# Seven block products for eight in the down projection of a two-layer transformer kernel

## The chip, the cores and the metric

The kernel runs on one core of a Trainium2 chip. The metric is the time of one execution on the device in microseconds (us), lower is better. The kernel before takes 3250.4 us, the median of three runs (3247.45 to 3253.56).

## What is computed

The model is a block of two stages. The first stage (mixers and a mixture of experts) is not touched. The second stage is two layers of the same form over x with 512 tokens and 1024 columns, all in 32-bit floats:

```python
def hybrid_layer(x, cond, ...):
    ...                                   # norm, four kinds of mixing heads, projection w_out
    x = x + gate1 * rms_norm(y, attn_post_g)
    h = rms_norm(x, mlp_pre_g) * (1.0 + scale2) + shift2
    y = jnp.square(jax.nn.relu(h @ mlp_w1)) @ mlp_w2      # 1024 -> 4096 -> 1024
    return x + gate2 * rms_norm(y, mlp_post_g)
```

The change is in the product with `mlp_w2`, the down projection: 512 x 4096 (activated tokens) times 4096 x 1024 (weights), once in each layer.

## The kernel before

The two layers are in the function `layers`. Each engine has its own program, written out by hand in order, and they meet at semaphores (`Signal`). Line numbers are those of the profile.

The activated tokens lie transposed in SBUF as `fT` (32 blocks of 128 hidden units, 512 tokens each). The weights stream through a ring of three slots of 2 MB (`RING`, `slot`, `take`), loaded by SyncE in the order of `tiles_of`: 27 tiles for each layer, the last 8 of them w1 and then 8 of w2, numbered from 0 to 7 in the down projection. `product` issues a matmul and reports a slot free to SyncE when the next tile is taken.

The up projection (`mlp_pe`, `pair_pe`, `mlp_dve`) already works with seven block products instead of eight: the operands are cut in two each way, sums of blocks are made on VectorE (`weight_sums_dve`, `token_sums_dve`), and its products are matmuls with 128x128 stationary weights and 256 moving token columns.

The down projection (`tensor_mlp`, `Back`) is a plain product. Tile m holds the weights of four hidden blocks (rows m*512 to m*512+511, all 1024 columns). For each block k, token tile t and column half, one matmul with stationary `fT` (128x128) and 512 moving weight columns adds into PSUM bank 2t + half, so all eight banks fill over all eight tiles. Only in the last tile (m = 7) is the order by token tile (`Back.tile_pe`), so that token tile 0 is complete while the others still run. Then, for each t: ScalarE takes the mean squares of both banks (`Back.squares`, L2779), VectorE adds them (`sums`, L2789), GpSimd takes the root (`pool`, L2785), and VectorE scales both halves with the gate and adds them to x (`Back.dve`, L2795 and L2797).

At the end of layer 0 this last tile is moved into the front of layer 1 (`tensor_front`): token tiles 0 to 2, the turn of the parameter vectors (`vectors_pe`, L2611), the transposes of the newly normalised token tile 0 (`norm1.pe(0)`, L2736), then token tile 3. Then the first input projection starts (`first_pe(0, 0)`). At the end of layer 1, the results are stored by SyncE token tile by token tile (L4106). The gate row of the layer (`gate_sp`, `gate_dve`) and a part of the constants that the up projection overwrites (columns `K_MASK` to `K_INV`) are loaded by SyncE in the down projection.

## Time and profile before

| | before |
|---|---|
| median of the runs | 3250.4 us |
| the profiled execution | 3247.82 us |
| its span, first to last instruction | 3246.0 us |
| TensorE busy | 2870.6 us, 88% |
| VectorE, ScalarE, GpSimd busy | 36%, 20%, 7% |
| mean granted TensorE clock | 0.924 of 2.4 GHz |
| down projection, layer 0 | 2110.5 to 2331.8 us |
| down projection, layer 1 | 3017.1 to 3236.9 us |

In the rows below a 32-bit matmul appears as two records. A row of the timeline gives the start, how long the merged records took, the engine, the line, and how many records there are; in square brackets stands the idle time before it and who ended it. Line 2570 is the line in `product`, so nearly all of the layers' matmuls have it: the operands (`ring_l,arena_l` for the down projection) and the shape tell them apart.

### The profile page before, as it was taken

Reading aid. Unit: us, or ns where it says so; the run is one execution under the profiler, and the core shown is the slowest. Engines: PE = TensorE matmul, PEld = TensorE weight load, DVE = VectorE, ACT = ScalarE, POOL = GpSimd, SP = SyncE. Lnnn points to the kernel's source line nnn. Section 1 sums busy time; section 2 is a strip of 40 time slices with the busy share of each in tenths; the row PEclk is TensorE's granted clock in tenths of the full one; section 3 lists DMA queues with packets and bytes.
Section 4 is the critical chain, followed back from the end, with each engine's and each line's share of the span. In section 5 each row is a group of like instructions: output and inputs, shape, how many; then the busy total and the mean of one; then the engine's idle time right before and its main releaser. Section 6 shows DMA issues by size and latency. Waiting matters only on the chain.

```text
span 3246.0 us, 38694 instructions
## 1 busy us (share of the span) xinstructions
PE 2870.6 (88%) x15675; PEld 1689.0 (52%) x15675; DVE 1177.9 (36%) x2584; ACT 652.0 (20%) x1504; POOL 241.2 (7%) x368
## 2 busy tenths in 40 slices
PE   6996888898888888669888899999998887999998
PEld 3544787453333333334646568744445465588543
DVE  3625454452111111428444167700255443333001
ACT  2133222011110110122222233300223123233000
POOL 0000000001111111102010011000020100000000
PEclk9998999999999998879985799999999875999999
DMA  6112444249999996531110035432211010222220
GB/s 215 52 53 104 165 152 171 83 163 376 407 412 402 400 398 268 214 116 53 39 40 27 30 144 213 185 116 78 94 53 40 13 53 6 72 78 101 101 78 26
DMA packets 138182, 469.76 MB, mean 145 GB/s; under 512 B 15341, under 2 KB 28299, under 8 KB 111895
## 3 DMA queue, kind: packets, MB, share of 16 engines
q1 hardware_dynamic: 118191, 416.29, 33.6%
q0 software_dynamic: 18912, 50.36, 4.2%
q8 instruction: 124, 2.03, 0.3%
q10 hardware_dynamic: 904, 0.66, 0.1%
q14 instruction: 51, 0.42, 0.0%
HBM read 460.90 MB, written 26.28 MB: 150 GB/s over the span
## 4 chain that ended last, share of the span: by engine, by line
PE 48%; DVE 5%; ACT 2%; issue 1%; SPq 0%; DMA 0%; POOL 0%; POOLq 0%; ACTq 0%; DVEq 0%
PE ps_l L2570 40%; PE ps_l L3049 2%; PE ps_l L76 2%; PE ps_l L3349 1%; PE ps_l L3251 1%; DVE pT_notsel_l L3026 1%; DVE small_l L3024 1%; DVE pT_notsel_l L3016 0%; PE ps_l L3131 0%; PE ps_l L159 0%; DVE small_l L3368 0%; ACT work_l L3112 0%; PE ps_l L2995 0%; PE ps_l L3258 0%; PE ps_l L2736 0%
## 5 line engine op out<-in xcount | busy, mean ns | idle before, releaser
L2570 PE MATMUL ps_l<-ring_l,hT_l 128*128 128x512 f32 (+3 forms) x1280 | 546.9, 575 | 12.1 <-ACT arena_l L2866 7.6
L2570 PE MATMUL ps_l<-ring_l,arena_l 128*128 128x512 f32 x1024 | 440.1, 592 | 0.7 <-ACT arena_l L168 0.7
L2570 PEld LDWEIGHTS ps_l<-ring_l,hT_l 128*128 128x128 f32 x1280 | 254.1, 209 | 234.9 <-issue 198.2
L2091 PE MATMUL ps_m<-w_m,gatheredT_m 128*64 128x512 f32 (+1 forms) x784 | 297.0, 651 | 48.7 <-issue 45.8
L2570 PEld LDWEIGHTS ps_l<-ring_l,arena_l 128*128 128x128 f32 x1024 | 194.4, 190 | 245.1 <-issue 243.5
L2570 PE MATMUL ps_l<-hT_l,ring_l 128*128 128x256 f32 (+1 forms) x1088 | 263.9, 394 | 6.0 <-ACT hT_l L2743 2.7
L2570 PEld LDWEIGHTS ps_l<-hT_l,ring_l 128*128 128x128 f32 x1088 | 205.5, 191 | 46.4 <-issue 10.7
L2091 PEld LDWEIGHTS ps_m<-w_m,gatheredT_m 128*64 128x64 f32 (+1 forms) x784 | 104.0, 165 | 178.2 <-issue 175.1
L369 PE MATMUL ps_a<-arena_a,ring_a 128*128 128x512 f32 (+2 forms) x496 | 169.7, 518 | 0.9 <-DVE arena_a L517 0.9
L2204 DVE TENSOR_TENSOR silu_m<-silu_m,ps_m 128x256 f32<-128x256 f32 x42 | 17.7, 421 | 373.4 <-ACT silu_m L2156 373.4
L2789 DVE SCALAR_TENSOR_TENSOR small_l<-small_l 128x1 f32<-128x1 f32 x16 | 2.5, 158 | 402.3 <-ACT work_l L2779 402.2
L2091 PE MATMUL ps_m<-hT_m,gatheredT_m 128*64 128x512 f32 (+1 forms) x272 | 134.0, 650 | 14.2 <-issue 13.9
L2115 PE MATMUL ps_m<-w_m,aT_m 128*64 128x512 f32 (+1 forms) x392 | 138.1, 597 | 0.7 <-DVE aT_m L2214 0.7
L369 PEld LDWEIGHTS ps_a<-arena_a,ring_a 128*128 128x128 f32 (+1 forms) x496 | 87.2, 182 | 83.8 <-issue 77.8
L2570 PE MATMUL ps_l<-consts_l,work_l 128*128 128x256 f32 x512 | 122.1, 381 | 5.9 <-DVE consts_l L3638 5.9
L2570 PEld LDWEIGHTS ps_l<-consts_l,work_l 128*128 128x128 f32 x512 | 96.3, 190 | 27.8 <-issue 15.2
L2156 ACT ACTIVATE silu_m<-ps_m 128x256 f32<-128x256 f32 x42 | 16.1, 383 | 437.8 <-PE ps_m L2091 437.8
L2779 ACT ACTIVATE work_l<-ps_l 128x512 f32<-128x512 f32 x32 | 18.8, 593 | 406.3 <-PE ps_l L2570 406.3
L130 DVE SCALAR_TENSOR_TENSOR gla_l<-pT_notsel_l,small_l,gla_l 128x256 f32<-128x256 f32 x168 | 81.4, 485 | 6.0
L2866 ACT ACTIVATE arena_l<-ps_l 128x512 f32<-128x512 f32 (+2 forms) x48 | 23.6, 492 | 257.6 <-PE ps_l L2570 257.6
L2210 DVE COPY rows_io_m<-ps_m 128x512 f32<-128x512 f32 x42 | 29.0, 691 | 122.2 <-PE ps_m L2115 122.2
L2091 PEld LDWEIGHTS ps_m<-hT_m,gatheredT_m 128*64 128x64 f32 (+1 forms) x272 | 42.4, 161 | 59.4 <-issue 58.6
(564 smaller groups left out, 3754.6 us busy)
## 6 DMA issues: line engine op xcount, KB each, us to landing
ring_l<-in_mlp_w SPq DMA_DIRECT2D x32, 2048.0 KB, 7.7
w_m<-in_exp_w_gate SPq DMA_DIRECT2D x49, 1024.0 KB, 13.2
w_m<-in_exp_w_up SPq DMA_DIRECT2D x49, 1024.0 KB, 16.1
w_m<-in_exp_w_down SPq DMA_DIRECT2D x49, 1024.0 KB, 13.1
ring_a<-in_mod_w SPq DMA_DIRECT2D x12, 2048.0 KB, 8.9
pT_notsel_l<-in_mod_w POOLq DMA_DIRECT2D x24, 1024.0 KB, 5.7
ring_a<-in_w_mod SPq DMA_DIRECT2D x9, 2048.0 KB, 8.8
hT_m<-in_exp_w_gate SPq DMA_DIRECT2D x17, 1024.0 KB
```

The source lines that it names most:

```text
L76: mm = self.nc.tensor.transpose(self.banks[n % len(self.banks)][0:src.shape[1], bank_cols], src, self.ident[0:src.shape[0], 0:src.shape[0]])
L130: dve.scalar_tensor_tensor(out, w[:, k, :], cond[:, k:k + 1], out, ALU.mult, ALU.add).then_inc(signal.sem, signal.up())
L369: mm = pe_.matmul(out, lhsT, rhs, start=start, stop=stop)
L2091: mm = pe_.matmul(PS[h * rows:(h + 1) * rows, 2, :], hg[s % 2][:, k, h * rows:(h + 1) * rows], gu_w[w][:, k, :, :], start=k == 0, stop=k = ...
L2115: mm = pe_.matmul(PS[h * rows:(h + 1) * rows, 4 + half, :], AT[:, at:at + rows], dn_w[w][:, k, half * 512:(half + 1) * 512], start=k == 0, ...
L2210: dve_.tensor_copy(YB[:, ring * D + 512:(ring + 1) * D], PS[:, 5, :]).then_inc(dn_ev_v.sem, 1)
L2570: mm = pe_.matmul(out, lhsT, rhs, start=start, stop=stop, **group)
L3024: dve_.max(top, nb[:, i, 0:s]).then_inc(own_v.sem, own_v.up())
L3026: dve_.match_replace(nb[:, i, 0:s], top, nb[:, i, 0:s], TAKEN).then_inc(own_v.sem, own_v.up())
L3049: mm = pe_.matmul(PS[:, 6, h * 64:(h + 1) * 64], src[:, j, h, :], proj[:, j, c:c + 64], start=j == 0, stop=j == i)
L3251: mm = pe_.matmul(PS[:, 2 * (n % 3) + h % 2, 0:P], a_, b_, start=True, stop=True, tile_position=(32 * h, 0))
L3349: pe_.matmul(PS[:, bank, 0:s], TB[o:o + 32, 2 + b, i * P:(i + 1) * P], TB[o:o + 32, 4 + b, 0:s], start=True, stop=True, tile_position=(o, 0))
```

## The change

The down projection of both layers becomes seven block products in place of eight. The hidden dimension is cut into even and odd blocks, the tokens into two halves of 256, and the columns are done in two passes q of 512, each cut into two halves of 256. A tile of w2 is now 1024 rows by 512 columns: tiles 0 to 3 are pass 0, 4 to 7 pass 1. For each tile (a "group" i) there are seven products, named 1, 2, 3, 6, 5, 7, 4 in the order of TensorE, each of eight matmuls (four hidden pairs, two token tiles) with a stationary token block or token sum and 256 moving columns. Each product has its own PSUM bank, which adds up over the four groups of a pass; `down_out_dve` combines the seven banks into four blocks of y, which go to SBUF. VectorE makes the token sums (four operations of 128x1024 in pass 0, two in pass 1) and the weight sums (four for each group, in place in the ring's slot, `b11` only after product 1 has read it).

The products 7 and 4 of the last group are the only ones left for the end (`down_tail_pe`); at the end of layer 0 they stand in the front of layer 1, before `norm1.pe(0)`. The mean squares are taken for each half of the columns; the gate's second addend is kept in `spare` and no longer in `work_l`; the reload of the constants moves from the down projection of layer 0 to SyncE's program after tile 2 of layer 1.

```diff
-            return out + [rows(p["w2"], m) for m in range(8)]
+            return out + [cols(p["w2"][g * KD * P:(g + 1) * KD * P, :], q * 512, (q + 1) * 512) for q in range(2) for g in range(4)]
...
+        DOWN_BANK = {"1": 6, "2": 0, "3": 1, "6": 4, "5": 3, "7": 2, "4": 5}
+        DOWN_OUT = ("11", "u2", "u4", "12", "u3", "22", "21")
...
 def vectors_pe(l):
-                pe_.wait_ge(back2.added.sem, NT * (l - 1) + 2)
+                pe_.wait_ge(down_added.sem, down_added.at(down_at("11", 1)))
...
+        class BackHalves(Back):
+            def half_squares(self, t, q):
+                act_.wait_ge(down_added.sem, down_added.at(down_at("12" if t < 2 else "21", q)))
+                act_.activation(SM[:, 1024 + q * 512:1536 + q * 512], y_half[q][:, t, :], ACT.Square, scale=1.0 / math.sqrt(D),
+                                accum_out=ms_b[:, 2 * t + q:2 * t + q + 1]).then_inc(self.sq.sem, self.sq.up())
+                act_.wait_ge(self.sq.sem, self.sq.n)
...
+        def down_group(x, i, stationary, moving):
+            for p in range(PAIRS_IN):
+                for u in range(2):
+                    mm = product(PS[:, DOWN_BANK[x], u * HT2:(u + 1) * HT2], stationary[:, p, u * P:(u + 1) * P], moving[:, p, :],
+                                 start=i % DG == 0 and p == 0 and u == 0, stop=i % DG == DG - 1 and p == PAIRS_IN - 1, skip_group_check=True)
+            mm.then_inc(down_mm[x].sem, down_mm[x].up())
...
+        def down_first_pe(l, i):
+            if i == DG:
+                pe_.wait_ge(down_part.sem, down_part.at(1))
+                pe_.wait_ge(down_added.sem, down_added.at(down_at("11", 0)))
+            take(hold=i == 2 * DG - 1)
+            if i == DG - 1:
+                pe_.wait_ge(m_ready.sem, m_ready.at(4 * PAIRS))
+            down_group("1", i, a11, b11)
+            down_group("2", i, a12, b21)
+            pe_.wait_ge(down_s.sem, down_s.at(s_count(i)))
+            if i == DG:
+                pe_.wait_ge(down_added.sem, down_added.at(down_at("21", 0)))
+            down_group("3", i, ds4[i % 2], b22)
+            pe_.wait_ge(down_t.sem, down_t.at(4 * i + 2))
+            ...
+            down_group("6", i, ds2[i % 2], dt2)
+            down_group("5", i, s1_, b11)
+        def down_last_pe(l, i):
+            pe_.wait_ge(down_t.sem, down_t.at(4 * i + 4))
+            down_group("7", i, a21, b12)
+            down_group("4", i, a22, b21)
+        def down_pe(l):
+            for i in range(2 * DG):
+                down_first_pe(l, i)
+                if i + 2 < 2 * DG:
+                    down_last_pe(l, i)
+            down_last_pe(l, 2 * DG - 2)
+            owed[0] = taken[0] - 1 - w_used.n
...
+        def down_tokens_dve(l, i):
+            if i < DG:
+                dve_.wait_ge(m_ready.sem, m_ready.at(relu_at["21", 4 * i + 3]))
+                dve_.tensor_tensor(s1_, a21, a22, ALU.add).then_inc(down_s.sem, down_s.up())
+                dve_.wait_ge(down_s.sem, down_s.n)
+            if i >= 2:
+                dve_.wait_ge(down_mm["6"].sem, down_mm["6"].at(i - 1))
+            dve_.tensor_tensor(ds2[i % 2], s1_, a11, ALU.subtract).then_inc(down_s.sem, down_s.up())
+            dve_.wait_ge(down_s.sem, down_s.n)
+            dve_.tensor_tensor(ds4[i % 2], a12, ds2[i % 2], ALU.subtract).then_inc(down_s.sem, down_s.up())
+            if i < DG:
+                dve_.tensor_tensor(a21, a11, a21, ALU.subtract).then_inc(down_s.sem, down_s.up())
+        def down_weights_dve(l, i):
+            dve_.wait_ge(w_loaded[n % RING].sem, 16 * (n // RING + 1))
+            dve_.wait_ge(down_mm["1"].sem, down_mm["1"].at(i + 1))
+            dve_.tensor_tensor(b11, b12, b11, ALU.subtract).then_inc(down_t.sem, down_t.up())
+            ...
+            dve_.tensor_tensor(dt2, b22, b11, ALU.subtract).then_inc(down_t.sem, down_t.up())
+            ...
+            dve_.tensor_tensor(b12, b22, b12, ALU.subtract).then_inc(down_t.sem, down_t.up())
+            dve_.wait_ge(down_mm["2"].sem, down_mm["2"].at(i + 1))
+            dve_.tensor_tensor(b21, b21, dt2, ALU.subtract).then_inc(down_t.sem, down_t.up())
+        def down_dve(l):
+            down_tokens_dve(l, 0)
+            for i in range(2 * DG):
+                down_weights_dve(l, i)
+                if i + 1 < 2 * DG:
+                    down_tokens_dve(l, i + 1)
+                if i == DG - 1:
+                    for which in DOWN_OUT:
+                        down_out_dve(which, 0)
+                if i == DG:
+                    gate_dve(2 * l + 1)
+                    ...
+            for which in ("11", "u2", "u4"):
+                down_out_dve(which, 1)
...
 def vector_front(l):                 # l = 1; the end of layer 1 has the same order without the norm1 and vectors steps
-                for t in range(2):
-                    back2.sums(t)
-                    back2.dve(t)
-                    norm1.dve(t)
-                vectors_dve(l)
-                ...
+                down_out_dve("12", 1)
+                vectors_dve(l)
+                back2.sums(0)
+                back2.sums(1)
+                down_out_dve("u3", 1)
+                down_out_dve("22", 1)
+                back2.dve(0)
+                down_out_dve("21", 1)
+                back2.dve(1)
+                back2.sums(2)
+                back2.sums(3)
+                for t in range(2):
+                    norm1.dve(t)
+                back2.dve(2)
+                norm1.high_dve(0)
+                ...
 def vector_attention(l):
+            dve_.wait_ge(ld_const.sem, 16 * (l + 1))
...
 def sync_program(sp):
                 if l >= 1 and r == 2:
                     sp.wait_ge(back2.added.sem, NT * l)
                     gate_sp(sp, l, 0)
+                    sp.dma_start(K[:, K_MASK:K_INV], consts[:, K_MASK:K_INV]).then_inc(ld_const.sem, ld_const.up(16))
```

## Rows read from the trace of the kernel before

**Rows 1.** The page: busy time of the engines, and the chain that ended last by engine
```profile
PE 2870.6 (88%) x15675; PEld 1689.0 (52%) x15675; DVE 1177.9 (36%) x2584; ACT 652.0 (20%) x1504; POOL 241.2 (7%) x368
PE 48%; DVE 5%; ACT 2%; issue 1%; SPq 0%; DMA 0%; POOL 0%; POOLq 0%; ACTq 0%; DVEq 0%
```

**Rows 2.** Stretches, layer 1: length, busy PE, PEld, DVE, ACT, POOL, clock, DMA share, GB/s
```profile
2870.00:2920.00 50.00, 50.00 (x233) 44.03 (x232) 15.88 (x30) 17.48 (x48) 0.00 (x0) 1.00 0.24 85
...
3063.00:3113.00 50.00, 50.00 (x118) 22.20 (x117) 0.00 (x0) 0.00 (x0) 0.00 (x0) 1.00 0.24 84
```

**Rows 3.** Timeline of TensorE, layer 1: first and last piece of the down projection
```profile
3017.05 18.19 PE L2570 MATMUL ps_l<-ring_l,arena_l 128*128 128x512 f32 x42
...
3224.76 12.18 PE L2570 MATMUL ps_l<-ring_l,arena_l 128*128 128x512 f32 x28
```

**Rows 4.** Timeline of TensorE, up projection: 64 records from the first to the last
```profile
2900.62 1.89 PE L2570 MATMUL ps_l<-hT_l,ring_l 128*128 128x256 f32 x8
...
2914.43 1.89 PE L2570 MATMUL ps_l<-consts_l,work_l 128*128 128x256 f32 x8
```

**Rows 5.** Timeline of VectorE: sums of the up projection, adds from PSUM
```profile
2905.10 0.68 DVE L3619 TENSOR_TENSOR work_l<-ring_l 128x512 f32<-128x512 f32 x1
...
3017.25 0.42 DVE L3647 TENSOR_TENSOR arena_l<-arena_l,ps_l 128x256 f32<-128x256 f32 x1 [3.29 <-PE ps_l L2570]
```

**Rows 6.** Timeline, end of layer 1: the last token tile after TensorE's end
```profile
3237.04 0.60 ACT L2779 ACTIVATE work_l<-ps_l 128x512 f32<-128x512 f32 x1 [5.60 <-PE ps_l L2570]
...
3238.34 0.16 DVE L2789 SCALAR_TENSOR_TENSOR small_l<-small_l 128x1 f32<-128x1 f32 x1 [3.39 <-ACT work_l L2779]
...
3239.16 1.41 DVE L2795 SCALAR_TENSOR_TENSOR pT_notsel_l<-ps_l,small_l,gates_l 128x512 f32<-128x512 f32 x2 [0.66 <-POOL small_l L2785]
3240.60 1.23 DVE L2797 TENSOR_TENSOR x<-x,pT_notsel_l 128x1024 f32<-128x1024 f32 x1
```

**Rows 7.** Timeline of TensorE, layer 0's down projection and the front of layer 1
```profile
2110.52 14.86 PE L2570 MATMUL ps_l<-ring_l,arena_l 128*128 128x512 f32 x34 [0.68 <-ACT arena_l L168]
...
2323.49 0.25 PE L2611 MATMUL ps_l<-consts_l,vrows_l 97*128 97x97 f32 x1
...
2324.90 7.03 PE L2570 MATMUL ps_l<-ring_l,arena_l 128*128 128x512 f32 x16
...
2332.65 13.15 PE L2570 MATMUL ps_l<-ring_l,hT_l 128*128 128x512 f32 x32
```

**Rows 8.** Timeline, same front: norm steps of ScalarE, GpSimd and VectorE
```profile
2314.99 1.06 ACT L2717 ACTIVATE work_l<-x 128x1024 f32<-128x1024 f32 x1 [3.71 <-DVE x L2797]
...
2316.54 0.57 POOL L2725 TENSOR_TENSOR small_l<-small_l 128x1 f32<-128x1 f32 x1
...
2317.14 0.75 DVE L2729 TENSOR_SCALAR pT_notsel_l<-x,small_l 128x1024 f32<-128x1024 f32 x1 [2.24 <-POOL small_l L2725]
...
2328.76 1.36 DVE L2750 TENSOR_SCALAR hT_l<-ps_l,modcols_l 128x128 f32<-128x128 f32 x4
```

**Rows 9.** Timeline of TensorE: a long gap, and the front of layer 0
```profile
2572.27 0.81 PE L3251 MATMUL ps_l<-gla_l 32*128 32x128 f32 x8 [7.18 <-DVE arena_l L3296]
...
1412.19 16.24 PE L2570 MATMUL ps_l<-ring_l,hT_l 128*128 128x512 f32 x32 [0.94 <-DVE hT_l L2750]
```

**Rows 10.** A stretch after that gap: length, TensorE busy, granted clock, DMA share, GB/s
```profile
2577.00:2578.00 1.00, 1.00 (x9) 0.50 0.00 0
```

**Rows 11.** DMA issues of the page: KB each, us from issue to landing
```profile
ring_l<-in_mlp_w SPq DMA_DIRECT2D x32, 2048.0 KB, 7.7
consts_l<-consts_layer SPq DMA_DIRECT2D x1, 1408.0 KB, 14.4
```

**Rows 12.** The chain that ended last, in order of time: top-k search of layer 1
```profile
2390.67 0.50 DVE pT_notsel_l L3016
```

**Rows 13.** Timeline of TensorE: start of the up projection in either layer
```profile
1894.67 3.69 PE L2570 MATMUL ps_l<-hT_l,ring_l 128*128 128x256 f32 x16 [1.36 <-ACT hT_l L2743]
...
2816.25 3.69 PE L2570 MATMUL ps_l<-hT_l,ring_l 128*128 128x256 f32 x16 [1.36 <-ACT hT_l L2743]
```

More of the change, by code:

```diff
@@ L2589, in vectors_sp @@
             sp.dma_start(WA[0:16, :], p["wa2"]).then_inc(ld_row.sem, ld_row.up(16))
-        gate_parts = [(a[:, 0:D], a[:, D:2 * D]) for a in (spare, SM)]
+        gate_parts = (spare[:, 0:D], spare[:, D:2 * D])
         def gate_sp(sp, l, g):
@@ L3662, in mlp_dve @@
             add_dve("21", PAIRS - 1)
-            gate_dve(2 * l + 1)
-        def tensor_front(l, w):
+        DG, PAIRS_IN, W2_FIRST = 4, 4, 19
+        halves = fT.rearrange("p (a o) t -> p a o t", o=2)
+        down_mm = {x: sig("down_p" + x) for x in DOWN_BANK}
+        down_s, down_t, down_part = sig("down_s"), sig("down_t"), sig("down_part")
+        part_1, part_u = [GL[:, n * 512:(n + 1) * 512].rearrange("p (u n) -> p u n", u=2) for n in range(2)]
+        dt2 = SM[:, 0:1024].rearrange("p (k n) -> p k n", k=4)
@@ new lines, in layers, with down_weights, down_tokens @@
+        ds2, ds4 = [[PN[:, n * 1024 + i * 2048:(n + 1) * 1024 + i * 2048].rearrange("p (k n) -> p k n", k=4) for i in range(2)] for n in range(2)]
+        def down_weights(l, i):
+            w = slot(l * PER + W2_FIRST + i).rearrange("p (a o) n -> p a o n", o=2)
+            return [w[:, :, o, h * HT2:(h + 1) * HT2] for o in range(2) for h in range(2)]
+        def down_tokens(g):
+            a = halves[:, g * PAIRS_IN:(g + 1) * PAIRS_IN]
+            s1_ = HT[:, g * 1024:(g + 1) * 1024].rearrange("p (k n) -> p k n", k=4)
+            return [a[:, :, o, h * HT2:(h + 1) * HT2] for h in range(2) for o in range(2)] + [s1_]
@@ L3668, in tensor_front @@
+        def tensor_front(l):
+            vectors_pe(l)
             if l:
-                for t in range(3):
-                    back2.tile_pe(fT, w, 7, t)
-            vectors_pe(l)
+                down_tail_pe(l - 1)
+                pe_.wait_ge(lam_ready.sem, l + 1)
             norm1.pe(0)
-            if l:
-                back2.tile_pe(fT, w, 7, 3)
-            pe_.wait_ge(lam_ready.sem, l + 1)
+            if l == 0:
+                pe_.wait_ge(lam_ready.sem, l + 1)
             norm1.pe(1)
@@ L3807, in tensor_mlp @@
             mlp_pe(l)
[L3808 to L3820 removed]
+            down_pe(l)
             if l == NL - 1:
[L3822 to L3824 removed]
+                down_tail_pe(l)
         def scalar_front(l):
@@ L3929, in scalar_mlp @@
                 nxt.wait_stored(act_)
+            down_part_act(0)
+            for t in range(NT):
+                back2.half_squares(t, 0)
+            if l + 1 < NL:
                 lam_act(l + 1)
-            else:
-                act_.wait_ge(gates_ready.sem, 2 * NL)
+            down_part_act(1)
+            if l + 1 == NL:
                 for t in range(NT):
-                    back2.squares(t)
+                    back2.half_squares(t, 1)
         def vector_front(l):
@@ L4032, in vector_mlp @@
             mlp_dve(l)
-            if l + 1 < NL:
-                lam_first_dve(l + 1)
-                lam_row_dve(l + 1)
-            else:
-                for t in range(NT):
-                    back2.sums(t)
-                    back2.dve(t)
+            down_dve(l)
+            if l + 1 == NL:
+                down_out_dve("12", 1)
+                back2.sums(0)
+                back2.sums(1)
+                down_out_dve("u3", 1)
+                down_out_dve("22", 1)
+                back2.dve(0)
+                down_out_dve("21", 1)
+                back2.dve(1)
+                back2.sums(2)
+                back2.sums(3)
+                back2.dve(2)
+                back2.dve(3)
         def gpsimd_front(l):
@@ L4048, in gpsimd_front @@
             else:
-                for t in range(NT):
-                    back2.pool(t)
+                back2.pool(0)
+                back2.pool(1)
+                norm1.pool(0)
+                back2.pool(2)
+                back2.pool(3)
+                for t in range(1, NT):
                     norm1.pool(t)
@@ L4107, in sync_program @@
             sp.wait_ge(stored.sem, 16 * NT)
-        closing = (back2.mm, back2.sq, back2.sum, back2.rs, back2.added)
-        w = None
+        closing = (back2.mm, back2.sq, back2.sum, back2.rs, back2.added, down_added, down_s, down_t, down_part, *down_mm.values())
         for l in range(NL):
```

107 lines of the change are left out of this document (69 added, 38 removed).

## The prediction

> **What bounds the kernel now.** I read the page first: TensorE is busy 88% of the span, VectorE 36%, and of the chain that ended last TensorE has 48% of the span, the next engine 5% [rows 1]. The share over the whole program is an average, so next I asked for busy time by stretch. In the down projection TensorE is busy 50.00 of 50 us at a granted clock of 1.00 (its upper level, 2.4 GHz), and VectorE, ScalarE and GpSimd do nothing at all; in the up projection TensorE is just as full, while VectorE works 15.9 of 50 us beside it [rows 2]. The reader is to see two things there: a matmul taken out of the down projection comes off the end, and three engines stand free to pay for it. The weights take 0.24 of the DMA engines' time, so they don't bind.
>
> The profiled execution took 3247.8 us (span 3246.0, and 1.8 around it), 2.6 us under the median of the three runs, 3250.4. I make the sum against the profiled one and put the difference of 2.6 back at the end.
>
> **Matmuls removed.** The down projection of layer 1 starts at 3017.05 and its last piece ends at 3224.76 + 12.18 = 3236.94 [rows 3]. That is 219.9 us for 8 tiles x 4 blocks x 4 token tiles x 2 halves = 256 matmuls, 512 records, so 0.4295 us a record of 512 columns. The change has 8 groups x 7 products x 8 matmuls = 448 matmuls, 896 records of 256 columns. Such a record stands in the trace: the up projection has the same form (stationary 128x128, 256 columns, a weight load before each), and from 2900.62 to 2914.43 it issues 64 of them in 13.81 us, 0.2158 each [rows 4]. So 896 x 0.2158 = 193.4 us, and a product (16 records) is 3.45. Halving the width costs almost nothing: two narrow records are 0.4316 against 0.4295. Gain: 26.5 us in each layer, 53.1 in both.
>
> A rule of the Trainium skill speaks against that: "TensorE: Matmul & The Clock Gate", section "Why this matters for your kernels", asks to keep all dimensions at 512 or more for target efficiency. By that rule narrow matmuls would lose part of the eighth; the 0.2158 of the up projection doesn't show such a loss, and I go by the row.
>
> **Sums on VectorE.** In pass 0 a group has 4 token and 4 weight operations, in pass 1 2 and 4, each 128x1024. An operation of 128x512 between the same kinds of operands takes 0.68 [rows 5], one of 128x1024 takes 1.23 [rows 6]; with the step to a dependent one I use 1.26. That is 10.1 us in a group that lasts 7 x 3.45 = 24.2 us on TensorE, and 7.6 in pass 1. Throughput is there 2.4 times over. The order has to fit as well. Product 6 needs two weight sums that begin when product 1 ends; between lie products 2 and 3, 6.9 us, against 2 x 1.26 = 2.5. Product 7 needs all four, 13.8 us after product 1, against 5.0. Product 3 needs the token sums, made a group ahead. Only the first group has no group ahead: its sums start after VectorE's last add of the up projection (3017.25 + 0.42 = 3017.67 [rows 5]) and end at 3022.7; product 3 is due at 3017.05 + 6.9 = 3023.95. Cover 1.2 us, so this is nothing, and if each operation took 1.6 instead of 1.26 it would just begin to cost. In layer 0 TensorE starts the down projection only after a copy of the parameter product on ScalarE (idle 0.68 us before it [rows 7]), which comes after that add, so the cover is no less. The end of pass 0 (a copy on ScalarE and seven adds of 128x512 from PSUM; two half-size ones take 0.42 each, so I use 0.75) hangs on product 4 only for the last add, "21". TensorE asks for "21" before product 3 of the next group, 6.9 us later: nothing. Behind those adds on VectorE wait the weight sums of group 4, whose own wait (product 1 of that group, 3.45 us later) is longer. The gate and the lambda steps stand on VectorE in group 4, about 4 us in a group with 12 us to spare.
>
> **Loads.** A w2 tile is still 2 MB with rows of 2 KB, the same shape as a w1 tile; the 32 tiles of both matrices land in 7.7 us at the median [rows 11], and they are asked for two groups (48 us) ahead. Nothing. The reload of the constants (1408 KB, 14.4 us to landing [rows 11]) moves behind the gate's three loads after tile 2 of layer 1, and the load of tile 3 waits behind it. VectorE now waits for it ahead of the top-k search, 58 us after the front starts (2390.67 [rows 12] against 2332.65 [rows 7]); asked for some 3 us into the front, it is there 40 us early. Tile 3 isn't asked for until its slot is free, in the same late part. Nothing.
>
> **The end of layer 0: a new wait.** Before, the last token tile's products (7.03 us) fill the time in which tile 0 is normalised. From 2110.52 to the first projection at 2332.65 there are 222.1 us, of which 219.9 are the down projection, 0.5 the vectors and 1.7 transposes: TensorE doesn't pause [rows 7]. After the change nothing of that kind is left, since the last products (7 and 4 of group 7) belong to all columns of a half. I count from the end of product 5 of group 7 (time 0). TensorE does 7 and 4 of group 6, the vectors, 7 and 4 of group 7, and ends at 4 x 3.45 + 0.6 = 14.6 with its restarts. VectorE goes on with "u3" once product 7 ends (11.1), "22" to 12.6, the closing steps of token tile 0 (1.41 + 1.23 + 0.03 = 2.67, [rows 6]) to 15.3, "21" to 16.0, tile 1 to 18.7, two small sums to 19.1 and the scaling of tile 0 (0.75, [rows 8]) to 19.8. ScalarE has squared tile 0 and the halves of tiles 2 and 3 by 18.2, tile 1 (1.06 and its readout) by 20.0; GpSimd gives that root at 21.0 (0.57 a power, three in a row, [rows 8]); VectorE scales tile 1 to 21.8, closes tile 2 to 24.5 and writes the upper half of hT for tile 0 (1.36, [rows 8]) to 25.9. Then the first projection can start. Of these 25.9 us TensorE works 14.4 + 2.1 for transposes = 16.5; it waits 9.4 us, against 0.2 before. Cost 9.2.
>
> **The clock there.** In layer 1 a pause of 7.18 us [rows 9] takes the clock to its lower level, 0.50 (1.2 GHz), still so 5 us after the matmuls resume [rows 10]. The front of layer 0 starts just so, out of a pause: its first 32 records take 16.24 us [rows 9], the same 32 in layer 1, warm, 13.15 [rows 7]. The new pause is 5.2 us, then 1 us of transposes, 1 us, transposes, 3 us. The bounds are 0 (no fall) and 3.1; I take 3.1, since the front of layer 0 is the nearest row, in pattern too. The same page, section "Why this matters for your kernels", warns of idle gaps between bursts of matmuls for this reason, and the trace agrees.
>
> So layer 0's stretch becomes 52 x 3.453 + 25.9 + 3.1 = 208.6 in place of 222.1: -13.5.
>
> **The end of layer 1.** Before, TensorE ends at 3236.94 and the span at 3246.0, 9.1 later: squares (0.60 each half), sum, root, closing steps of one token tile (to 3241.83), store (4.2) [rows 6]. After, in the same count without the vectors: product 4 ends at 13.8; "u3", "22" from 10.4 to 11.9; tile 0 to 14.6; "21" to 15.3; tile 1 to 18.0; two sums and the root to 19.0; tile 2 to 21.7; tile 3 to 24.3; store to 28.5. The tail is 14.7 long, three token tiles in a row on VectorE where one was. Cost 5.6; layer 1's stretch becomes 193.4 + 14.7 = 208.1 in place of 3246.0 - 3017.05 = 228.95: -20.9.
>
> **Sum.** -13.5 - 20.9 = -34.4. 3247.8 - 34.4 = 3213.4 for the profiled execution, 3216.0 as a median. The middle part of layer 1 shifts 13.5 us earlier; it has phases at the lower clock, but its length hardly depends on them: from the first projection to the up projection it is 482.5 us in layer 0 and 483.6 in layer 1 (1412.19 to 1894.67 [rows 9, 13], 2332.65 to 2816.25 [rows 7, 13]), 3.1 of the former for its cold start. So I allow 4 us either way.
>
> **The rivals.**
> A. The clock stays up through the broken pause. For: transposes lie in it, and the later pauses are shorter. Against: 5.2 us come first, and 7.18 was enough [rows 9]. Time 3216.0 - 3.1 = 3212.9.
> B. The two ends cost twice what I count, because the norm chain crosses four engines and I may have missed steps or its later token tiles hold TensorE again. For: VectorE has about 26 us of strictly ordered work there. Against: after the first projection starts, 13 us of matmuls cover tiles 2 and 3. Price 9.2 + 5.6 once more: 3230.8.
> C. The other side, slower than before: TensorE waits in every group for VectorE's sums. The place is `down_s` and `down_t` before products 3, 6 and 7. The price of x us an operation beyond the cover is 8x - 24.2 in each of 4 groups and 6x - 24.2 in the other 4, 112x - 387 in both layers. It loses the 34.4 and 6.5 more from x = 3.8 us, giving 3257. The strided views (four runs of 256) could be slower than the contiguous 1.23, but 0.68 for four runs of 128 in the up projection is already the strided case, so three times that is hard to believe.
> D. The change doesn't do what it says for TensorE: a narrow record costs more in this mix, the weight load no longer hidden (the loads are 44 of 50 us in the up projection [rows 2]). At 0.225 instead of 0.2158 both layers lose 16.5: 3232.5. Against it, the same shape in the up projection.
>
> **How the numbers follow.** A measurement of this kernel can tell about 0.2%, 6.5 us, from no change. Forecast 3216 with 0.58 (3210 to 3222); A 0.17; B 0.13; D 0.07; C 0.03; 0.02 for a loss that just eats the gain. All but C and the last are faster by over 6.5 us: faster 0.95, same 0.02, slower 0.03. The range goes from A less 4 us of the middle part and 2 of the two ends (3207) up to B with a little over (3231).
>
> **What would show it right or wrong.** In the profile after: 896 narrow records in each down projection at 0.216 from start to start; TensorE busy 50 of 50 there with VectorE near 20; VectorE 128x1024 near 1.25; a pause of some 5 us and one of some 3 around the transposes at layer 1's front, with 16 us for the first 32 records; 14 to 15 us from TensorE's end to the span's. Wrong would be idle time of TensorE released by VectorE inside the groups, a narrow record over 0.22, or a middle part of layer 1 outside 480 to 490 us.

## The result and the profile after

The changed kernel takes 3202.6 us in its first measurement (median of three, 3198.7 to 3216.5), a ratio of 0.9866 to the kernel before (95% interval 0.9827 to 0.9905): faster, by far more than the 6.5 us that the prediction took as the least that can be told. A fourth execution, in a slow state at a mean granted clock of 0.55, took 4866 us and isn't counted. The forecast was 3216, a ratio of 0.9894, with a range of 3207 to 3231. The ratio forecast lies inside the interval; the measured time lies 4 us below the range. In a second measurement of the same kernel, six runs against sixteen of the kernel before, the ratio is 0.9894 (0.9874 to 0.9915). That this is the ratio forecast to the last digit is partly luck: the interval is some 13 us wide.

The profiled execution took 3202.6 us (the sum gave 3213.4), and its span is 3200.8. Busy time and the chain by engine, on the page of the changed kernel, answer to [rows 1]:

```profile
PE 2814.4 (88%) x16443; PEld 1833.8 (57%) x16443; DVE 1329.2 (42%) x2724; ACT 655.8 (20%) x1508; POOL 244.0 (8%) x368
PE 46%; DVE 7%; ACT 2%; issue 1%; SPq 0%; DMA 0%; POOL 0%; ACTq 0%; DVEq 0%; POOLq 0%
```

TensorE has 56 us less, VectorE 151 us more, and the chain is still TensorE's. One stretch in each down projection (length; busy time of TensorE, its weight loads, VectorE, ScalarE, GpSimd; granted clock; DMA share and GB/s), to be read beside [rows 2]:

```profile
2150.00:2200.00 50.00, 50.00 (x233) 44.02 (x232) 19.36 (x18) 1.44 (x4) 0.00 (x0) 1.00 0.24 85
3050.00:3100.00 50.00, 50.00 (x233) 44.01 (x232) 23.04 (x24) 3.49 (x9) 0.00 (x0) 1.00 0.24 85
```

The down projection now looks like the up projection: 233 records in 50 us, TensorE full, VectorE in the middle of its work. The timeline of a group (start, us, engine, line, shapes, count) shows the sums beside the products:

```profile
2159.70 1.23 DVE L3805 TENSOR_TENSOR ring_l<-ring_l 128x1024 f32<-128x1024 f32 x1 [14.51 <-PE ps_l L2570]
2160.96 1.22 DVE L3807 TENSOR_TENSOR work_l<-ring_l 128x1024 f32<-128x1024 f32 x1
2162.22 1.22 DVE L3809 TENSOR_TENSOR ring_l<-ring_l 128x1024 f32<-128x1024 f32 x1
2162.88 3.62 PE L2570 MATMUL ps_l<-ring_l,pT_notsel_l 128*128 128x256 f32 x16
2163.36 1.22 DVE L3811 TENSOR_TENSOR ring_l<-ring_l,work_l 128x1024 f32<-128x1024 f32 x1
2164.50 1.22 DVE L3789 TENSOR_TENSOR hT_l<-arena_l 128x1024 f32<-128x1024 f32 x1
...
2166.34 3.62 PE L2570 MATMUL ps_l<-work_l,pT_notsel_l 128*128 128x256 f32 x16
...
2169.79 3.62 PE L2570 MATMUL ps_l<-ring_l,hT_l 128*128 128x256 f32 x16
```

A product lasts 3.45 us from start to start, a sum 1.26. L3807 makes the weight sum for product 6; it ends at 2162.2 and product 6 (`work_l,pT_notsel_l`) starts at 2166.3, without a wait. VectorE waited 14.51 us for TensorE before the group.

The front of layer 1, TensorE, answers to [rows 7]:

```profile
2107.53 7.17 PE L2570 MATMUL ps_l<-ring_l,arena_l 128*128 128x256 f32 x32 [0.68 <-ACT arena_l L168]
...
2294.60 7.17 PE L2570 MATMUL ps_l<-ring_l,arena_l 128*128 128x256 f32 x32
2306.96 4.03 PE L2747 MATMUL ps_l<-consts_l,pT_notsel_l 128*128 128x128 f32 x16 [5.19 <-DVE pT_notsel_l L2740]
2312.97 14.69 PE L2570 MATMUL ps_l<-ring_l,hT_l 128*128 128x512 f32 x32 [1.98 <-DVE hT_l L2761]
```

The pause is there, 5.19 us before the transposes and 1.98 after them, and the transposes run at the lower clock (4.03 us for 16 records, against 1.91 for 16 warm ones later in the front). By the microsecond (length, TensorE busy, granted clock, DMA share, GB/s):

```profile
2303.00:2304.00 1.00, 0.00 (x0) 1.00 0.00 0
2305.00:2306.00 1.00, 0.00 (x0) 0.85 0.00 0
2307.00:2308.00 1.00, 1.00 (x5) 0.50 0.00 0
2314.00:2315.00 1.00, 1.00 (x3) 0.50 0.00 0
2316.00:2317.00 1.00, 1.00 (x3) 1.00 0.79 117
```

The end of layer 1, after TensorE's last product (3172.74 + 13.98 = 3186.72), answers to [rows 6]:

```profile
3172.74 13.98 PE L2570 MATMUL ps_l<-ring_l,arena_l 128*128 128x256 f32 x64
...
3187.28 0.68 DVE L3782 TENSOR_TENSOR arena_l<-gla_l,ps_l 128x512 f32<-128x512 f32 x1
...
3189.32 1.23 DVE L2829 TENSOR_TENSOR x<-x,pT_notsel_l 128x1024 f32<-128x1024 f32 x1
...
3192.72 1.23 DVE L2829 TENSOR_TENSOR x<-x,pT_notsel_l 128x1024 f32<-128x1024 f32 x1
...
3195.30 1.22 DVE L2829 TENSOR_TENSOR x<-x,pT_notsel_l 128x1024 f32<-128x1024 f32 x1
```

The three additions to x shown close token tiles 1, 2 and 3, one after another behind TensorE, and the span ends 14.1 us after it.

**Where the 45.2 us between the two spans came from.** The boundaries are the first projection of each layer, the start of its up projection and the start of its down projection, all read from TensorE's timeline (for before [rows 3, 7, 9, 13]):

| stretch | before | after | difference | forecast |
|---|---|---|---|---|
| start to layer 0's first projection | 1412.2 | 1409.2 | -3.0 | 0 |
| middle of layer 0 (to the up projection) | 482.5 | 482.5 | 0.0 | 0 |
| up projection of layer 0 | 215.8 | 215.8 | 0.0 | 0 |
| down projection and front, to layer 1's first projection | 222.1 | 205.4 | -16.7 | -16.6 |
| middle of layer 1, its cold start included | 483.6 | 479.4 | -4.2 | +3.1 |
| up projection of layer 1 | 200.8 | 200.8 | 0.0 | 0 |
| down projection and end of layer 1 | 228.95 | 207.6 | -21.3 | -20.9 |

The two stretches of the down projections agree with the sum within half a microsecond. The surprise is in two that the change doesn't touch (the first stage and the middle of layer 1), and in the price of the cold start, which the table counts in the latter. The 479.4 us of that middle lie outside the 480 to 490 that the prediction gave as a sign of being right.

### The profile page after: what moved, and what is told of

Its sections match the earlier page's. It is cut to its first block, busy times and chain, and to the rows that moved or that the text cites. A ratio compares the mean times of both kernels' runs of the same rounds, so it can differ in the third digit from the quotient of the medians.

```text
span 3200.8 us, 40435 instructions
## 1 busy us (share of the span) xinstructions
PE 2814.4 (88%) x16443; PEld 1833.8 (57%) x16443; DVE 1329.2 (42%) x2724; ACT 655.8 (20%) x1508; POOL 244.0 (8%) x368
## 4 chain that ended last, share of the span: by engine, by line
PE 46%; DVE 7%; ACT 2%; issue 1%; SPq 0%; DMA 0%; POOL 0%; ACTq 0%; DVEq 0%; POOLq 0%
PE ps_l L2570 38%; PE ps_l L3081 2%; PE ps_l L76 2%; DVE pT_notsel_l L3058 1%; DVE small_l L3056 1%; PE ps_l L3381 1%; PE ps_l L3283 1%; DVE pT_notsel_l L3048 1%; PE ps_l L3163 0%; PE ps_l L159 0%; DVE small_l L3400 0%; ACT work_l L3144 0%; PE ps_l L3290 0%; PE ps_l L3117 0%; DVE pT_notsel_l L2827 0%
## 5 line engine op out<-in xcount | busy, mean ns | idle before, releaser
L2570 PE MATMUL ps_l<-ring_l,hT_l 128*128 128x512 f32 (+3 forms) x1536 | 602.3, 541 | 13.8 <-ACT arena_l L2898 7.3
L2570 PEld LDWEIGHTS ps_l<-ring_l,hT_l 128*128 128x128 f32 x1536 | 301.5, 205 | 242.4 <-issue 200.0
L2570 PE MATMUL ps_l<-ring_l,arena_l 128*128 128x256 f32 x1024 | 224.3, 379 | 0.7 <-ACT arena_l L168 0.7
L3805 DVE TENSOR_TENSOR ring_l<-ring_l 128x1024 f32<-128x1024 f32 x16 | 19.6, 1225 | 174.9 <-PE ps_l L2570 174.9
L2115 PEld LDWEIGHTS ps_m<-w_m,aT_m 128*64 128x64 f32 (+1 forms) x392 | 45.2, 152 | 53.1 <-issue 51.1
```

Source lines behind the costliest of these rows:

```text
L2115: mm = pe_.matmul(PS[h * rows:(h + 1) * rows, 4 + half, :], AT[:, at:at + rows], dn_w[w][:, k, half * 512:(half + 1) * 512], start=k == 0, ...
L2570: mm = pe_.matmul(out, lhsT, rhs, start=start, stop=stop, **group)
```

## The experiments

All of them are edits of the changed kernel, except where said. A profile of each gives the same stretches again, which turned out to be as useful as the edits.

**again**: the changed kernel, unedited. 

> The changed kernel once more, unedited. The first measurement gave 3202.6 us for the profiled execution where the sum gave 3213.4; by stretches the two down projections and their ends agree with the sum within 2 us, and 3.0 us come from the first stage and 4.2 us from the middle of layer 1, both untouched. Theory 1: these 7 us are scatter of untouched stages, not of the change. Then over more rounds the ratio settles near (3250.4 - 35)/3250.4 = 0.989, and in this profile the first stage ends between 1409 and 1413 us and the middles of the two layers lie anywhere from 479 to 485 us. Theory 2: the change itself shortens the middle of layer 1. Then the ratio stays at 0.986 to 0.987 and the middle of layer 1 is again near 479 us.

Measured: ratio 0.9894 (0.9874 to 0.9915), six runs from 3204.3 to 3227.0, median 3208.6 against 3247.5. The first stage ended at 1415.1, the middles took 479.36 and 479.44, the down projection and front 205.44 again. Theory 1 stands as far as the ratio goes, and its scatter was still put too small: 1415.1 lies outside the 1409 to 1413 expected. The middle of layer 1 is where theory 2 wanted it, so only the profiles of the other runs can decide between the two.

**narrow**: the kernel before, with each down matmul cut in two (the edit in short form).

```diff
-                return product(PS[:, 2 * t + half, :], src[...], w[:, k, half * 512:(half + 1) * 512], ...)
+                for c in range(0, 512, 256):
+                    mm = product(PS[:, 2 * t + half, c:c + 256], src[...], w[:, k, half * 512 + c:half * 512 + c + 256], ...)
```

> The kernel before with each matmul of the down projection cut into two of 256 columns: 1024 records a layer instead of 512, eight products' worth of work. Theory 1 (width costs only what the up projection's record shows): 1024 x 0.2158 = 221.0 us a layer against 219.9, +2 us in all. Rival (narrow matmuls cost more where 128x128 weights are loaded for each): 0.225 us a record would give +10 us a layer.

Measured: ratio 1.002 (1.0006 to 1.0033). From the down projection to layer 1's first projection 223.4 us instead of 222.1, in layer 1 from its down projection (3010.54) to the end 230.3 instead of 228.95: +1.3 in each, +2.6 in all. Width costs 1.3 ns for each narrow record (1.3 us over 1024), not 10. The stretch in layer 0:

```profile
2150.00:2200.00 50.00, 50.00 (x234) 44.01 (x233) 0.59 (x6) 0.20 (x1) 0.00 (x0) 1.00 0.23 85
```

The same rate as after, with VectorE idle.

**eight**: an eighth product in each group.

```diff
             down_group("5", i, s1_, b11)
+            for p in range(PAIRS_IN):
+                for u in range(2):
+                    product(PS[:, 7, u * HT2:(u + 1) * HT2], s1_[:, p, u * P:(u + 1) * P], b11[:, p, :], ...)
```

> The changed kernel with an eighth product in each group (8 matmuls more, product 5 repeated into the free bank 7, its result unused). It gives the price of one block product. Theory 1: 8 groups x 16 records x 0.2158 = 27.6 us a layer, +55.2 us in all, and the down projections take 221.1 us, within 1.3 of the kernel before. Rival (part of the eighth is hidden or a product costs more where VectorE works beside it): anything 3 us from that.

Measured: ratio 1.0064 (1.0039 to 1.0089) to the kernel before. From down projection to first projection 2346.21 - 2113.14 = 233.07 us, and in layer 1 from 3029.91 to TensorE's end at 3251.09 221.18 us; against the changed kernel's 205.44 and 193.55 that is +27.63 in each layer, +55.3 in all. The price of a block product is fully paid or fully gained, 3.45 us each, and the whole scheme without the saved product loses to the plain one: by 18.5 us in the medians, most of it at its two ends (10.9 us more from the down projection to layer 1's first projection, 6.3 more from layer 1's down projection to the end of the span, of which narrow puts 1.3 each down to width).

**no_sums**: all token and weight sums left out; TensorE's waits for them are gone too, products 3, 6 and 5 take plain blocks instead, and the seven bank results are combined as before, so the result is no longer the down projection.

```diff
-            down_group("3", i, ds4[i % 2], b22)
+            down_group("3", i, a12, b22)
...
-            down_group("6", i, ds2[i % 2], dt2)
-            down_group("5", i, s1_, b11)
+            down_group("6", i, a11, b22)
+            down_group("5", i, a21, b11)
...
-            down_tokens_dve(l, 0)
...
-                down_weights_dve(l, i)
```

> The changed kernel without any token or weight sum of the down projection and without TensorE's waits for them; products 3, 6, 5 take plain blocks, so what it computes is not the down projection. Theory 1 (the sums lie wholly beside TensorE's work): the two down projections keep their 193.5 us, the total changes by less than 1 us. Rival (VectorE's 80 us of sums a layer slow TensorE, by waits at the first product 3 or by sharing memory): the down projection gets shorter by some us, a record falls under 0.2158 us.

Measured: median 3208.5, ratio 0.9906 (0.9878 to 0.9934), not to be told from the changed kernel. The profile is sharper: 205.43 us from down to first projection with the sums gone, 205.44 with them, and in layer 1

```profile
3000.00:3050.00 50.00, 50.00 (x234) 44.01 (x233) 0.00 (x0) 0.00 (x0) 0.00 (x0) 1.00 0.34 120
```

the same rate in 50 us with VectorE at 0 (234 records against 233), and 193.55 us for the down projection with or without sums. The sums cost TensorE nothing.

**double**: each of the sums issued twice in a row (an in-place sum is applied twice, so the values change; the first of them shown).

```diff
+                dve_.tensor_tensor(s1_, a21, a22, ALU.add).then_inc(own_v.sem, own_v.up())
+                dve_.wait_ge(own_v.sem, own_v.n)
                 dve_.tensor_tensor(s1_, a21, a22, ALU.add).then_inc(down_s.sem, down_s.up())
```

> The changed kernel with each token and weight sum of the down projection issued twice in a row on VectorE (in-place sums are applied twice, so the values differ from the reference's). A sum step then takes 2.5 us in place of 1.25. By the prediction's cover: product 3 of the first group is due 6.9 us after the start of the down projection, its sums end 0.6 + 8 x 1.26 = 10.7 us after it in layer 1, so TensorE pauses 3.8 us there, and 0.8 us in layer 0, where VectorE is free 3 us earlier; every later group has 16 x 1.26 = 20 us of sums in 24.2 us and product 6 waits for 5.0 us of sums under 6.9, so none pauses. Theory 1: +4.6 us, and up to 1.5 more if the clock falls in the pause. Rival (cover shorter than counted, waits in each group): +10 us or more, with idle time of TensorE in every group.

Measured: median 3216.2, ratio 0.9886 (0.9838 to 0.9934). In layer 0 206.93 us instead of 205.44, in layer 1 198.95 from 2995.01 to TensorE's end instead of 193.55: +1.5 and +5.4, 6.9 in all, a little over the 4.6 to 6.1 expected. TensorE's timeline in layer 1 and in layer 0:

```profile
2995.01 7.07 PE L2570 MATMUL ps_l<-ring_l,arena_l 128*128 128x256 f32 x32
3005.52 5.41 PE L2570 MATMUL ps_l<-ring_l,pT_notsel_l 128*128 128x256 f32 x16 [3.43 <-DVE arena_l L3805]
...
2112.08 3.63 PE L2570 MATMUL ps_l<-ring_l,pT_notsel_l 128*128 128x256 f32 x16
2116.91 3.72 PE L2570 MATMUL ps_l<-work_l,pT_notsel_l 128*128 128x256 f32 x16 [1.20 <-DVE work_l L3819]
```

The pause is in the first group only, 3.43 us before product 3 in layer 1, and the product after it takes 5.41 us instead of 3.62, at the lower clock for a part. In layer 0 the pause was where the count had none, 1.20 us before product 6: there the sums of tokens end in time, but the weight sums stand behind them. No later group waits. So the cover computed in the prediction is real, and thinnest at the start of a down projection. The clock took more here than elsewhere as well: the first 32 records of layer 1's first projection needed 15.88 us in this profile, against 14.69 in that of the changed kernel.

**fill** and **fill2**: dummy matmuls into the free bank 7 in the pauses of the front of layer 1. fill has the first two of these, fill2 all three.

```diff
+                for _ in range(11):
+                    pe_.matmul(PS[:, 7, 0:256], ident, K[:, K_ID:K_ID + 256], start=True, stop=True)
             norm1.pe(0)
+                for _ in range(2): ...
             norm1.pe(1)
+                for _ in range(6): ...
```

> The changed kernel with 11 dummy matmuls of 256 columns (22 records, 4.7 us) on TensorE in its pause before the transposes of layer 1's first token tiles, and 2 (0.9 us) after the first of them. VectorE's chain there stays as it is. Theory 1 (the pause lets the clock fall, which costs 1.5 us in the first 32 records of the projection): the granted clock stays at 1.00 through the front, those records take 13.2 us instead of 14.7, and the projection still starts 205.4 us after the down projection. Rival: the clock falls all the same, or the dummies delay the front by what they save.

Measured: the projection started 205.44 us after the down projection, but its first 32 records took 14.92 us. The clock was 1.00 through the filled pauses and fell after the last open one:

```profile
2343.30 14.92 PE L2570 MATMUL ps_l<-ring_l,hT_l 128*128 128x512 f32 x32 [2.85 <-DVE hT_l L2761]
```

and by stretches of 3 us (length, TensorE busy, clock, DMA share, GB/s)

```profile
2340.00:2343.00 3.00, 0.44 (x5) 1.00 0.00 0
2343.00:2346.00 3.00, 2.70 (x4) 0.55 0.00 0
```

My expectation missed: 2.85 us of pause is enough here, where 5.19 had been. Hence the second one. (The total, 3215.5, says nothing on it, see below.)

> The dummies once more, now in all three pauses of the front of layer 1: 11 dummy matmuls of 256 columns before the first transposes, 2 between, 6 (2.6 us) after the second ones, where the last pause of 2.85 us stayed open and the clock fell. Theory 1 (any open pause there lets the clock fall, a filled one doesn't): granted clock 1.00 from the end of the down projection into the projection, its first 32 records in 13.2 us, the projection starting 205.4 us after the down projection. The gain of 1.5 us is below what the total can show; the profile decides. Rival (something other than the pauses lowers the clock, such as the loads that start with the projection): again 14.7 us or more.

Measured: ratio 0.9852 (0.9823 to 0.9881), and in the profile (TensorE's timeline, then the stretch around its first row)

```profile
2318.73 13.22 PE L2570 MATMUL ps_l<-ring_l,hT_l 128*128 128x512 f32 x32 [0.26 <-DVE hT_l L2761]
```

```profile
2316.00:2320.00 4.00, 3.74 (x15) 1.00 0.00 0
```

with the projection again 205.44 us after the down projection. The pauses are what lowers the clock, and against the profile of the changed kernel filling them is worth 14.7 - 13.2 = 1.5 us. The loads that start with the projection don't lower it.

**early**: the ends reordered. Token tiles 0 and 1 need no result of products 7 and 4. Shown is VectorE's part at the front of layer 1 and TensorE's; the end of layer 1 and the steps of ScalarE and GpSimd are reordered to match.

```diff
                 down_out_dve("12", 1)
-                vectors_dve(l)
                 back2.sums(0)
                 back2.sums(1)
+                back2.dve(0)
+                back2.dve(1)
+                vectors_dve(l)
+                for t in range(2):
+                    norm1.dve(t)
                 down_out_dve("u3", 1)
                 down_out_dve("22", 1)
-                back2.dve(0)
+                norm1.high_dve(0)
                 down_out_dve("21", 1)
-                back2.dve(1)
...
 def down_tail_pe(l, between):
             down_group("7", i, a21, b12)
+            between()                  # norm1.pe(0) at the head of layer 1
             down_group("4", i, a22, b21)
```

> The changed kernel with its two ends reordered. Token tiles 0 and 1 need only products 1, 2, 3, 6 and 5, so VectorE closes them (and scales them for the next norm) before it waits for product 7; TensorE does the transposes of tile 0 between products 7 and 4 of the last group. Theory 1 (the pause of 7.2 us and the clock's fall in the front of layer 1 come only from the order on VectorE): the first projection starts 16.5 us after product 5 of the last group instead of 25.8, its first 32 records take 13.2 us instead of 14.7, and the end of layer 1 takes 12.3 us after TensorE's last product instead of 14.1. Sum -12.7 us against the changed kernel, some 3190 us. Rival (the norm chain across the engines holds the front whatever the order): less than 3 us are gained.

Measured: median 3197.8, ratio 0.9852 (0.9839 to 0.9865). TensorE at the front of layer 1:

```profile
2294.47 3.72 PE L2570 MATMUL ps_l<-ring_l,arena_l 128*128 128x256 f32 x16
...
2298.03 1.04 PE L2747 MATMUL ps_l<-consts_l,pT_notsel_l 128*128 128x128 f32 x8
2298.90 3.62 PE L2570 MATMUL ps_l<-ring_l,arena_l 128*128 128x256 f32 x16
...
2302.36 1.04 PE L2747 MATMUL ps_l<-consts_l,pT_notsel_l 128*128 128x128 f32 x8
```

No pause is left, the projection follows 2303.23 - 2107.40 = 195.83 us after the down projection (-9.6) at full clock (13.15, -1.5), and the end after TensorE is 11.9 us (3192.1 - 3180.21), -2.2. Sum -13.3, expected -12.7; by the medians of the two kernels in the same measurement 10.8. The pause came from the order of the steps: nothing was taken out of any engine's program. How much of it VectorE's order alone gives back isn't shown, since the four engines were reordered together.

**early2**: early, and in the end of layer 1 the product of y with the gate made ahead (the second halves of the columns shown, the first ones stand before "u3").

```diff
+                back2.gated(2, 1)       # xn = y * gate, while ScalarE squares
+                back2.gated(3, 1)
                 back2.sums(2)
                 back2.sums(3)
-                back2.dve(2)
-                back2.dve(3)
+                back2.close(2)          # x = xn * root + x, one operation of 128x1024
+                back2.close(3)
```

> The reordered kernel, and in the end of layer 1 the closing step of token tiles 2 and 3 is cut in two: y times the gate is made while ScalarE squares, and one operation of 128x1024 then scales and adds to x. Theory 1 (VectorE's operations after the last product are the end's chain): the closing of a tile takes 1.3 us instead of 2.6, the end after TensorE's last product 9.7 us instead of 11.9, total about 2.2 us under the reordered kernel, ratio to the kernel before 0.984 to 0.986. Rival (the stores of two tiles at once, or GpSimd's roots, take VectorE's place): less than 1 us.

Measured: median 3195.3, ratio 0.9823 (0.9798 to 0.9849), the lowest median of all. TensorE's end at 3169.89 + 13.98 = 3183.87, span 3193.5: 9.6 us. The two closing steps:

```profile
3186.64 2.48 DVE L2839 SCALAR_TENSOR_TENSOR x<-pT_notsel_l,small_l,x 128x1024 f32<-128x1024 f32 x2 [0.29 <-POOL small_l L2796]
```

The mechanism is as expected in the profile; the ratios of early and early2 overlap, so the 2.3 us between them rest on the profile only.

## Why the prediction was right and where it was wrong

**Matmuls removed: right.** 896 narrow records took 193.55 us (2993.17 to 3186.72) where the sum had 193.4; eight confirms the price of a product, narrow that of the width. The advice of the Trainium skill to keep all dimensions at 512 or more ("TensorE: Matmul & The Clock Gate", section "Why this matters for your kernels") is given there for the dimensions of a whole product, which no run here varies; the prediction read it as a rule for the width of a single matmul. Read so, it would have misled: the loss from width is 1.3 us a layer against 27.6 gained.

**Sums on VectorE: right, and bounded.** 1.22 to 1.23 us each as in [rows 6], no wait in any group, nothing gained without them. Doubling them costs 6.9 us, and only in the first group; rival C, which needed 3.8 us an operation, is far away. The step put the thin place at product 3 and overlooked product 6 in layer 0, which cost nothing here.

**Loads: right.** No wait of VectorE in layer 1 is for the reload of the constants, TensorE waited for no load in either down projection, and the 32 weight tiles landed in 8.2 us at the median, against 7.7 before.

**The front of layer 1: right.** The pause was counted as 5.2 and measured as 5.19, the projection was to start 205.5 us after the down projection and did so after 205.43 or 205.44 in five profiles (after, again, no_sums, fill, fill2). The 1 and 3 us of pause counted behind it came out as 1.98, since the slower transposes filled the rest; in fill, where they ran warm, the last pause is 2.85.

**The clock there: mechanism right, price from a single case.** I took layer 0's cold start, 3.1 us, as the price of a fall. In layer 1 the first 32 records took 14.69 us (after), 14.68 (again), 14.75 (eight), 14.91 (no_sums) and 15.88 (double), against 13.15 warm: 1.5 to 2.7 us. The cold start of layer 0 isn't fixed either, 15.97 to 16.25 us in ten profiles and 14.67 in double. Slow transposes stand ahead of both, so they don't explain the difference (below, layer 0 in before, then layer 1 in double; the rows of after, 4.03 and 14.69, stand in the section on the result):

```profile
1409.28 1.97 PE L2736 MATMUL ps_l<-consts_l,pT_notsel_l 128*128 128x128 f32 x8 [0.83 <-DVE small_l L2644]
...
2305.99 4.02 PE L2747 MATMUL ps_l<-consts_l,pT_notsel_l 128*128 128x128 f32 x16 [5.19 <-DVE pT_notsel_l L2740]
2312.00 15.88 PE L2570 MATMUL ps_l<-ring_l,hT_l 128*128 128x512 f32 x32 [1.99 <-DVE hT_l L2761]
```

What differs is when the clock came back: 3.0 us into the projection in after, 5.4 in double. No run shows what decides it. Rival A is refuted: the clock does fall.

**The end: right within 0.6.** 14.1 us against 14.7; three closing steps of 2.6 to 2.7 us, as counted, and shorter steps between them.

By the sum of the touched stretches the change gave -16.7 + 1.5 - 21.3 = -36.5 us, against -34.4. Of the 10.8 us that the profiled execution was below its forecast, this accounts for 2.1. The other 8.7 lie in untouched stretches: 3.0 in the first stage and 5.7 in the middle of layer 1 (it was 4.2 shorter than before, although 1.5 of cold start stand in it).

**The range: wrong.** The step that failed is "So I allow 4 us either way". It compared two middles of one profile, 482.5 and 483.6, and took their closeness for steadiness ("its length hardly depends on them"), and it allowed nothing for layer 0's middle and for the first stage. Eleven profiles, in which these stretches are the same but for the order of a few norm steps at the start of layer 1's middle, give:

| kernel | first stage ends | middle of layer 0 | middle of layer 1 |
|---|---|---|---|
| before | 1412.2 | 482.5 | 483.6 |
| after | 1409.2 | 482.5 | 479.4 |
| again | 1415.1 | 479.4 | 479.4 |
| no_sums | 1412.4 | 482.3 | 476.3 |
| narrow | 1409.3 | 479.3 | 481.9 |
| early | 1406.0 | 485.6 | 482.6 |
| double | 1409.9 | 479.3 | 482.2 |
| eight | 1414.8 | 482.5 | 482.9 |
| fill | 1416.2 | 505.8 | 483.3 |
| fill2 | 1412.0 | 485.5 | 483.2 |
| early2 | 1409.6 | 488.9 | 479.3 |

The first stage scatters by 10 us, layer 0's middle by 10 (26 with fill), layer 1's by 7. The 483.6 us from which the sum started are the longest middle of layer 1 in the table, though no cold start stands in them: the profile before was at the long end there, so a shorter one was the likelier outcome. Theory 2 of the run again isn't needed. Layer 0's middle, ahead of any change, scatters in the same way, and the changed kernels have middles of layer 1 from 476.3 to 483.3 where the two of the old form have 483.6 and 481.9. With two profiles of the old form a difference of 2 us can't be excluded.

What makes a middle long is the granted clock. Added up over stretches of 0.5 us, TensorE spent 136 to 139 us of layer 0's middle at its lower level in the three profiles of 479.3 to 479.4 us, 142 to 146 in the four of 482.3 to 482.5, 152 in the two of 485.5 to 485.6, 159 in early2 and 197 in fill. The middle of layer 0, in fill and in again (columns as above, all engines):

```profile
1416.18:1921.98 505.80, 448.92 (x1760) 265.92 (x1760) 220.20 (x571) 118.08 (x266) 51.47 (x98) 0.81 0.10 34
```

```profile
1415.10:1894.46 479.36, 422.64 (x1761) 244.71 (x1761) 220.01 (x571) 118.13 (x266) 51.45 (x98) 0.86 0.11 36
```

VectorE, ScalarE and GpSimd did the same work in the same time; TensorE took 26 us more for the same records, at a mean clock of 0.81 instead of 0.86. Most of it is lost in one stretch of 80 us (TensorE's columns):

```profile
1576.18:1616.18 40.00, 36.19 (x155) 0.62 0.09 27
1616.18:1656.18 40.00, 37.59 (x146) 0.70 0.08 26
```

```profile
1575.10:1615.10 40.00, 35.29 (x246) 0.96 0.09 27
1615.10:1655.10 40.00, 29.07 (x105) 0.93 0.09 27
```

In fill TensorE was at its lower level there for most of the time and got through 301 records where in again it did 351. In both the clock fell just after the same pause of 3.50 us. In again it was back some 3 us later, in fill only after some 55 us, although TensorE was busy in nearly all of them:

```profile
1589.10:1591.10 2.00, 2.00 (x20) 1.00 0.47 105
```

```profile
1612.18:1614.18 2.00, 2.00 (x11) 0.50 0.00 0
```
By the end of the pause of 7.2 us that follows (1678.21 in fill, 1654.03 in again) fill was 23.1 us behind; the other 3.3 came later.

Dense stretches show none of this: the up projection of layer 0 took 215.84 or 215.85 us in every one of the profiles. The clock of the middles before, 0.85 and 0.84, was to be had from the trace, and with it the warning; the size of the scatter was not, since that takes several profiles. In hindsight, with some 5 us for each of the three stretches (read off the table) and about 9 for the three together if they are independent, the low end would have been 3212.9 - 9 - 2 = 3202, just under the first median of 3202.6. The nine runs of both measurements have 3206.9, 0.1 us under the range; with three runs, where in the scatter the median falls is luck.

## What to carry to other kernels

Price a block product by the narrow matmul that already stands in the trace, and then ask what the removed work was covering: here 53 us came off TensorE and 17 of them went back at the two places where everything waits for the last product. Order the steps after a sum of products by what each result really needs; closing the half of the tokens that doesn't need the last two products regained 13 of the 17. And take the uncertainty of a total from the stretches at a changing clock, however far they are from the edit; for a small effect compare the edited stretch in the profiles, not the totals.

## What the runs showed of the hardware

In fill the clock fell at about the moment when TensorE resumed after a pause of 2.85 us: 1.00 up to 2343.0, 0.55 on average over the next 3 us. With that pause filled too, pauses of 0.19 to 0.35 us left it at 1.00 (fill2). The length of the pause doesn't settle it alone. The same pause of 0.86 us in layer 0's middle, with the same matmuls on both sides, was followed by a fall in after (0.56 on average over the 2 us from 1605.7) and by none in again (1.00):

```profile
1604.14 5.46 PE L3081 MATMUL ps_l<-arena_l 128*128 128x64 f32 x32 [0.86 <-DVE arena_l L3180]
```

```profile
1610.21 3.79 PE L3081 MATMUL ps_l<-arena_l 128*128 128x64 f32 x32 [0.86 <-DVE arena_l L3180]
```

The lengths of the middles are not spread evenly: 476.3, 479.3 to 479.4, 481.9 to 483.6, 485.5 to 485.6, 488.9, about 3.1 us apart, and so are several ends of the first stage (1406.0, 1409.2, 1412.2, 1415.1). For one such step the two rows above show the cause: those 32 records and the 12 after them took 3.35 us longer in after (5.46 and 4.65 us, against 3.79 and 2.97), and its middle of layer 0 is 3.1 us longer (482.5 against 479.4). One more spell at the lower clock made that step. Which pauses become such a spell in a given execution, and how long it lasts (3 or 55 us after the same pause of 3.50 us, in again and in fill), stays open.
